# In the first join, VectorE modulates the odd pairs of tiles and ScalarE only the even ones

## The reference, cut to what matters

```
h = h + g1 * rms_norm(y, norm_g[i, 1])
f = conv_ffn(rms_norm(h, norm_g[i, 2]) * (1.0 + sc2) + sh2, ...)
h = h + g2 * rms_norm(f, norm_g[i, 3])
```

## Time and profile before

| what | value |
|---|---|
| median of 3 runs | 2930.1 us (2927.53 to 2930.76) |
| the profiled execution, its own time | 2928.23 us |
| its span, first to last instruction | 2926.2 us |
| PE busy | 2717.0 us, 93% |
| DVE busy | 2066.7 us, 71% |
| ACT busy | 1279.0 us, 44% |
| POOL busy | 132.0 us, 5% |
| mean granted TensorE clock | 0.968 |

### The profile page before, as it was taken

One profiled execution on the slowest core, in us unless ns is written; L12 is line 12 of the kernel. 1 busy time (PEld: TensorE's weight loads), 2 busy tenths in 40 slices (PEclk: granted clock), 3 DMA queues, 4 the chain that ended last, 5 costly groups with the idle time before them and its releaser, 6 DMA issues. The chain is left out here.

```text
span 2926.2 us, 45016 instructions
## 1 busy us (share of the span) xinstructions
PE 2717.0 (93%) x17388; PEld 2452.2 (84%) x17388; DVE 2066.7 (71%) x2901; ACT 1279.0 (44%) x1906; POOL 132.0 (5%) x177
## 2 busy tenths in 40 slices
PE   6989786999999989999999989998999999999996
PEld 5979685999998979999997767776989989778785
DVE  4999998988976576555758676665577558684565
ACT  4232244443445343333443567776453334443333
POOL 0000000000000000000000003332000000000000
PEclk7999898999999989999999989999999999999998
DMA  7556310223222212232223210000222332333332
GB/s 297 195 193 221 105 58 29 83 84 94 86 81 65 73 58 87 79 94 86 80 80 94 80 58 1 2 1 8 81 86 87 93 101 87 94 113 103 101 94 85
DMA packets 66519, 263.14 MB, mean 90 GB/s; under 512 B 6960, under 2 KB 7216, under 8 KB 60080
## 3 DMA queue, kind: packets, MB, share of 16 engines
q1 hardware_dynamic: 58368, 213.17, 23.6%
q0 software_dynamic: 5760, 41.95, 4.1%
q10 hardware_dynamic: 2224, 5.69, 0.6%
HBM read 256.58 MB, written 4.19 MB: 89 GB/s over the span
## 5 line engine op out<-in xcount | busy, mean ns | idle before, releaser
L1749 PE MATMUL PS<-a_hi,w_hi 128*128 128x322 f32 (+7 forms) x3584 | 918.0, 325 | 78.9 <-DVE a_lo L1087 60.4
L1749 PE MATMUL PS<-a_lo,w_hi 128*128 128x322 f32 (+7 forms) x3584 | 897.5, 319 | 0.0
L1749 PE MATMUL PS<-a_hi,w_lo 128*128 128x322 f32 (+7 forms) x3584 | 896.1, 318 | 0.0
L1749 PEld LDWEIGHTS PS<-a_hi,w_hi 128*128 128x128 f32 x3584 | 609.7, 191 | 136.4 <-issue 78.3
L1749 PEld LDWEIGHTS PS<-a_lo,w_hi 128*128 128x128 f32 x3584 | 613.1, 192 | 26.8 <-issue 4.8
L1749 PEld LDWEIGHTS PS<-a_hi,w_lo 128*128 128x128 f32 x3584 | 611.0, 191 | 24.4
L1003 DVE TENSOR_TENSOR w_lo<-raw,w_hi 128x1024 fp32r<-128x1024 f32 (+2 forms) x380 | 445.1, 1171 | 195.0 <-ACT w_hi L497 191.3
L497 ACT ACTIVATE w_hi<-raw 128x1024 fp32r<-128x1024 f32 (+2 forms) x380 | 385.9, 1016 | 0.3 <-DMA raw<-wstream 0.2
L1749 PE MATMUL PS<-z_hi,w_hi 128*128 128x320 f32 (+1 forms) x1056 | 300.6, 339 | 30.0 <-DVE z_lo L1446 27.9
L1749 PE MATMUL PS<-z_lo,w_hi 128*128 128x320 f32 (+1 forms) x1056 | 298.1, 337 | 0.0
L1749 PE MATMUL PS<-z_hi,w_lo 128*128 128x320 f32 (+1 forms) x1056 | 298.0, 336 | 0.0
(11 more groups left out here) (249 smaller groups left out, 3127.2 us busy)
## 6 DMA issues: line engine op xcount, KB each, us to landing
raw<-wstream SPq DMA_DIRECT2D x380, 512.0 KB, 3.6
ada_slot<-adastream POOLq DMA_DIRECT2D x40, 1024.0 KB, 5.3
ada_first<-adastream SPq DMA_DIRECT2D x4, 2048.0 KB, 19.8
h<-xT SPq DMA_DIRECT2D x1, 2640.0 KB, 14.5
h<-xT ACTq DMA_DIRECT2D x1, 2480.0 KB, 13.3
out<-h ACTq DMA_DIRECT2D x1, 2048.0 KB, 9.3
out<-h SPq DMA_DIRECT2D x4, 512.0 KB, 2.8
rope_sb<-rope ACTq DMA_DIRECT2D x1, 1024.0 KB, 4.9
```

The costliest lines, as they stand in the source:

```text
L1749: last = MM(PS[:, 2 * j + m, 0:n], wt[:, j, k, :], mv[:, k, m * n:(m + 1) * n], start=(k == 0 and p_ == 0), stop=(k == tiles - 1 and p_ == 2))
```

## The change

ScalarE's loop over the pairs calls `modulate` only for m = 0 and 2, and `high_part` for all four. VectorE's `join_tail` gets, for the first join alone and for m = 1 and 3, a call of the new `join_modulate` between the normalising of pair m and the remainder of pair m - 1. It waits until `in_modulated` says that the pair before has been modulated, so that the counter rises in order, and for VectorE's own normalising; then two multiply-adds (`tensor_scalar` with a scale and a bias read for each partition) modulate the pair in place.

```
@@ -692,7 +692,8 @@
                     root(s + 4, MIX, 2)
                     for m in range(4):
                         tiles = join_tiles(x, m)
-                        modulate(x["n"], m, tiles, 0, 1, x["t0"])
+                        if m % 2 == 0:
+                            modulate(x["n"], m, tiles, 0, 1, x["t0"])
                         high_part(x["n"], m, tiles)
                         if m == 1:
                             split(q0, 1)
@@ -1144,6 +1145,16 @@
                     last = STT(hk, y[:, o:o + n], mod[x["layer"]][:, cnd, at_gate:at_gate + 1], hk, ALU.mult, ALU.add)
                 last.then_inc(h_updated, 1)
 
+            def join_modulate(x, m):
+
+                assert x["t0"] + x["w"] <= LAT
+                dve.wait_ge(in_modulated, 4 * x["n"] + m)
+                dve.wait_ge(in_normed, 4 * x["n"] + m + 1)
+                for k in range(2):
+                    tile, f = join_tiles(x, m)[:, k], 24 + 2 * m + k
+                    last = TS(tile, tile, mod[0][:, 0, 8 + f:9 + f], mod[0][:, 0, f:f + 1], ALU.mult, ALU.add)
+                last.then_inc(in_modulated, 1)
+
             def join_tail(x, q, begun=0):
 
                 for m in range(begun, 5):
@@ -1153,6 +1164,8 @@
                             dve.wait_ge(in_lo, 4 * x["n"] + m - 1)
                         TT(join_tiles(x, m), h[:, 2 * m:2 * m + 2, x["t0"]:x["t0"] + x["w"]], two_rms(x["w"]),
                            ALU.mult).then_inc(in_normed, 1)
+                    if x["y"] == "zA" and m in (1, 3):
+                        join_modulate(x, m)
                     if m:
                         remainder(x["n"], m - 1, join_tiles(x, m - 1))
                     if m == 2:
```

## The result

The changed kernel takes 2938.04 us (median of 22 runs, 2926.14 to 2941.56) against 2930.01 us before (22 runs, 2925.72 to 2933.32): the ratio is 1.0024, with a 95% interval of 1.0017 to 1.0030. The forecast was 2929.7 us and no difference. It is some 7 to 8 us slower, and the runs lie in two groups: 18 of 22 between 2935.8 and 2941.6, 4 between 2926.1 and 2928.9. So the median says where most runs are, and what has to be explained is why a second group came up.

A forecast was written before the change was run, and what follows sets the result against it. TensorE, 93% busy, was taken to be held at the first join by late low parts of the activations. The median 2930.1 us less a 0.35 us gain there was rounded to 2929.7 us, range 2927.0 to 2932.4.

The forecast's parts named there:

- What bounds the kernel: At the first join, 480 to 515 us, TensorE waits only for low parts of the activations: three waits, 12.8 us together.
- the relay: At the first join ScalarE and VectorE wait on each other in turn, which makes the low parts late; VectorE idles 1.70 us.
- J1 in VectorE's idle: Pair 1's two multiply-adds on VectorE, 485.60 to 486.75, fit its 1.70 us of idle and cost nothing, by 0.13 us.
- R2 late: Pair 2's remainder on VectorE starts at 494.90, 1.09 us later, so tiles 4 and 5 start at 496.46 instead of 495.37.
- R3 early and behind R2: Pair 3's remainder on VectorE directly follows pair 2's, 496.32 to 497.82, releasing tile 6 0.70 us earlier, at 497.88.
- no wait ahead of tile 6: Tiles 4 and 5 end at 498.35, past tile 6's release at 497.88, so TensorE has no third wait at the join.
- The gain at the spot: At the first join tiles 6 and 7 end at 500.12, where the next unit started at 500.47: 0.35 us gained.
- The wait ahead of tile 4: At the first join TensorE idles 1.36 us here, where it had 0.27 and 1.15 us in two places.
- The step that failed: Behind the join, from 500 us, TensorE is 97% busy for a hundred microseconds, so the 0.35 us reach the end.
- The rival of the falling clock: The clock falls in the 1.36 us gap ahead of tile 4; 1.6 us more for tiles 6 and 7, 2931.3 us; chance 0.14.
- The relay as a whole on the path: At the join all 3.5 us of two pairs leave ScalarE's path; gain capped at 1.42 us, 2928.7 us; chance 0.06.
- the higher price: At the join a pair on VectorE costs 1.74 us instead of 1.15: 0.7 us slower, 2930.8 us; chance 0.08.

The follow-up runs named there:

- early delay: Kernel before with sixteen one-column copies on VectorE ahead of the first chunk's last remainder, at about 52 us: 2928.64 us, ratio 1.0002.

## Why the prediction was wrong

**What bounds the kernel** was read rightly, and so was the relay: J1 in VectorE's idle, R2 late, R3 early and behind R2, no wait ahead of tile 6, all came as put. The pair on VectorE costs 1.14 us (1.15 forecast), and one multiply-add takes 609 to 618 ns, as the row of 617 had it. The estimate of 492 ns, worked out from "VectorE: DVE Perf Modes" of the Trainium skill, "Side-by-side: where the cycles go for N=2048 bf16", does not agree with that. The gain at the spot is 0.31 us (0.35 forecast). The wait ahead of tile 4 is 2.80 us and not 1.36, since in this execution the clock rose 3.0 us after tile 0 instead of 6.1; since tile 4 waits for R2 in either case, that changes nothing for what follows.

**The step that failed** is this one: "what follows waits on its results, so the 0.35 us go through to the end". A shift was taken for something that passes through a 97% busy TensorE unchanged. The runs show that it meets a clock whose changes are not shifted with it, and that the term which the sum put at nothing, the falls behind 500 us, is far larger than the gain: 4.3 us for the three of the first half (restart to restart) and 4.8 us in the second half of the profiled execution, against 0.31. 0.3 us less cost 8 us, 0.3 us put back brought them back, and a delay of 1 us in the kernel before costs as much without any of the change. With that step the chances fell too: 0.02 for slower was worked out from cases that all lay at the join.

**The rival of the falling clock** named the right mechanism and looked at one idle only, the one that the change makes. That one (2.80 us) brought no fall in the changed kernel. The idles of 2.58 us at the groups' ends, and that of 3.12 us ahead of 1253.89 in the second half, were in the profile of before, longer than the 1.91 us on which the rival rested, and stood with the clock at 1.00. I had the row of the feed-forward stage at 97% and didn't ask where the missing 3% lay in it. A fall at one of them costs 1.3 to 1.5 us; the prediction had 1.6 us for a fall at the join.

**The relay as a whole on the path** and **the higher price** didn't come: R2 was late as read, and the price was as read.

**The range** was made from the spread of the runs, 3.2 us in three of them. With 22 runs the kernel before itself spans 7.6 us, and the changed one 15.4.

**What stays open.** Each trace is one execution, and both traces of the changed kernel are of the upper group; a trace of its lower group would test the step in distance Q directly. What sets the 1.3 us of difference ahead of the join was not looked for. And that the stretches at the low level ahead of the join pull every execution back to the same distance from the clock's changes is supported but not shown step by step. In its favour: the early delay was absorbed, and the last fall ahead of tile 0 stands 7.2 to 7.6 us ahead of it in all 14 traces, although tile 0 itself starts anywhere from 487.5 to 491.8 us. First before, then after:

```profile
480.00:481.00 1.00, 0.00 (x0) 0.00 (x0) 1.00 (x1) 0.00 (x0) 0.00 (x0) 1.00 0.00 0
481.00:482.00 1.00, 0.00 (x0) 0.00 (x0) 1.00 (x1) 0.00 (x0) 0.00 (x0) 0.52 0.00 0
482.00:488.00 6.00, 0.00 (x0) 0.00 (x0) 4.26 (x4) 4.14 (x5) 0.00 (x0) 0.50 0.00 0
```

```profile
482.00:483.00 1.00, 0.00 (x0) 0.00 (x0) 1.00 (x1) 0.00 (x0) 0.00 (x0) 0.78 0.00 0
483.00:489.00 6.00, 0.00 (x0) 0.00 (x0) 5.39 (x6) 3.86 (x4) 0.00 (x0) 0.50 0.00 0
```

By these the clock falls at 481.0 and at 482.6, 7.5 and 7.3 us ahead of tile 0 (488.55 and 489.84); the trace with the early copies has 7.2.

## What to carry to other kernels

A change that moves a program by a few tenths of a microsecond can cost or give back many times that where TensorE has idles of two or three microseconds that come back at regular distances: here 0.3 us moved the median by 8 us. Look for them in the profile of before, even where the clock stands at full there, and count them as a risk of both signs. Look at the single runs, and not only at the median, since two groups mean two courses of the clock; and to test a small loss, put the shift back with work that does nothing before looking for a cause in the edit. Filling such idles with products that nobody reads gave the same time at both alignments tried (2929.0 and 2929.3 us), though not a shorter one than the good alignment; where TensorE had no idle, the filling cost 1.9 us.

## What the runs showed of the hardware that was not expected

The same idle of 2.58 us, at the same place of the program, leaves the granted clock at 1.00 in one execution and brings it to 0.50 in another. The share of runs that are hit goes from 0 of 22 to 18 of 22 over 0.3 us of shift. In the traces the outcome at the first such idle follows without an exception from how long before its end the clock had last fallen ahead of the join: 89.2 to 89.4 us a fall, 89.5 to 90.4 none, 90.6 and more a fall. And the same 1.06 us of delay is free at 52 us, where many falls and rises of the clock follow, and costs 7.6 us at 498, where none follows for 70 us.
